# The shift of the norms on ScalarE and VectorE alone, and a weight split moved behind the variance, in a four-layer diffusion backbone on one core

## What is computed

```python
mod_c = (sc @ ada_w[i] + ada_b[i]).reshape(6, D_MODEL)
hc = _rmsnorm(xc, norm_w[i, 0]) * (1.0 + mod_c[1]) + mod_c[0]
...
xc = xc + mod_c[2] * oc
hc = _rmsnorm(xc, norm_w[i, 1]) * (1.0 + mod_c[4]) + mod_c[3]
xc = xc + mod_c[5] * _conv_ffn(hc, ffn_w_up[i], ffn_conv_w[i], ffn_conv_b[i], ffn_w_down[i])
```

## Time and profile before

| what | us |
|---|---|
| median of 3 runs | 1853.62 |
| lowest and highest of them | 1853.53 and 1855.74 |
| the profiled execution | 1852.23 |
| its span | 1850.4 |
| busy: TensorE | 1800.7 |
| busy: VectorE | 1389.0 |
| busy: ScalarE | 986.3 |
| busy: GpSimd | 176.0 |

### The profile page before, as it was taken

The page is one execution under the profiler, slowest core; times in us unless marked ns, Lnnn a source line. Parts: engine busy times, 40 slices in busy tenths (PEclk is TensorE's granted clock), DMA queues, the critical chain, the costliest instruction groups (busy, mean ns, idle before and its releaser), DMA issues.

```text
span 1850.4 us, 27379 instructions
## 1 busy us (share of the span) xinstructions
PE 1800.7 (97%) x11032; PEld 1497.5 (81%) x11032; DVE 1389.0 (75%) x2064; ACT 986.3 (53%) x1492; POOL 176.0 (10%) x147
## 2 busy tenths in 40 slices
PE   5999999999999989999999999999999999999998
PEld 2988877798888867888977678888888787878888
DVE  3865677668898766999855588988765777769984
ACT  2754444545674454766445466744654445547763
POOL 2100121001000113000101110002100220020001
PEclk8999999999999999999999999999999999999999
DMA  8565656867656757675574776566555645545542
GB/s 369 193 229 194 213 206 227 317 231 283 258 217 216 285 207 288 255 290 189 215 299 179 296 290 277 201 224 258 212 197 175 228 180 213 176 165 200 194 175 84
DMA packets 74175, 421.28 MB, mean 228 GB/s; under 512 B 12384, under 2 KB 18936, under 8 KB 26432
## 3 DMA queue, kind: packets, MB, share of 16 engines
q1 hardware_dynamic: 55440, 392.98, 56.8%
q10 hardware_dynamic: 18608, 26.55, 4.3%
HBM read 408.51 MB, written 10.96 MB: 227 GB/s over the span
## 4 chain that ended last, share of the span: by engine, by line
PE 88%; DVE 6%; issue 2%; ACT 2%; DMA 1%; POOL 1%; POOLq 0%; DVEq 0%; ACTq 0%; SPq 0%
PE ps L652 18%; PE ps L674 9%; PE ps L709 9%; PE ps L655 9%; PE ps L634 6%; PE ps L690 5%; PE ps L712 4%; PE ps L637 3%; PE ps L753 3%; PE ps L620 3%; PE ps L622 3%; PE ps L621 3%; DVE spl_lo L498 1%; DMA raw<-in_stream 1%; PE ps L960 1%
## 5 line engine op out<-in xcount | busy, mean ns | idle before, releaser
L498 DVE TENSOR_TENSOR spl_lo<-raw,spl_hi 128x1024 fp32r<-128x1024 f32 x556 | 691.2, 1269 | 150.8 <-ACT spl_hi L487 149.3
L487 ACT ACTIVATE spl_hi<-raw 128x1024 fp32r<-128x1024 f32 x556 | 574.1, 1053 | 286.8 <-PE ps L712 109.5
L652 PE MATMUL ps<-H,spl_hi 128*128 128x512 f32 x1408 | 444.3, 397 | 3.7 <-DVE H L1847 2.4
L655 PEld LDWEIGHTS ps<-H,spl_lo 128*128 128x128 f32 x1408 | 264.5, 188 | 62.5
L655 PE MATMUL ps<-H,spl_lo 128*128 128x256 f32 x1408 | 276.7, 278 | 0.0
L652 PEld LDWEIGHTS ps<-H,spl_hi 128*128 128x128 f32 x1408 | 214.3, 189 | 18.5 <-issue 16.5
L709 PE MATMUL ps<-G,spl_hi 128*128 128x512 f32 x528 | 165.8, 395 | 0.0
L634 PE MATMUL ps<-B,spl_hi 128*128 128x512 f32 x512 | 160.8, 395 | 0.0
L620 PE MATMUL ps<-H,spl_hi 128*128 128x256 f32 x512 | 149.1, 291 | 5.8 <-DVE H L1852 3.3
L621 PE MATMUL ps<-H,spl_hi 128*128 128x256 f32 x512 | 146.0, 285 | 0.0
L622 PE MATMUL ps<-H,spl_lo 128*128 128x256 f32 x512 | 146.0, 285 | 0.0
(11 more groups left out here) (255 smaller groups left out, 2944.3 us busy)
## 6 DMA issues: line engine op xcount, KB each, us to landing
raw<-in_stream SPq DMA_DIRECT2D x366, 1024.0 KB, 5.0
out_new_C<-c_stage ACTq DMA_DIRECT2D x16, 512.0 KB, 3.8
column<-in_ada_cols SPq DMA_DIRECT2D x16, 512.0 KB, 5.3
ada_b<-in_ada_b ACTq DMA_DIRECT2D x4, 768.0 KB, 9.5
cond_all<-cond_out ACTq DMA_DIRECT2D x3, 1024.0 KB, 4.9
E<-rows_out ACTq DMA_DIRECT2D x8, 256.0 KB, 4.3
Em<-rows_out ACTq DMA_DIRECT2D x8, 256.0 KB, 4.6
x<-in_x ACTq DMA_DIRECT2D x1, 1024.0 KB, 11.7
```

Source lines behind the costliest of these rows:

```text
L487: act.activation(spl_hi[m % SPL][:, :], raw[r % RAW][:, h * HALF:(h + 1) * HALF], ACT.Copy).then_inc(S["hi_done"], 1)
L498: dve.tensor_tensor(spl_lo[m % SPL][:, :], raw[r % RAW][:, h * HALF:(h + 1) * HALF], spl_hi[m % SPL][:, :].bitcast(F32), ALU.subtract).the ...
L652: pe.matmul(banks[:, b * 512:(b + 1) * 512], spl_hi[m % SPL][:, c], H[:, kk * 512:(kk + 1) * 512], start=kk == 0, stop=False, skip_group_c ...
L655: mm = pe.matmul(banks[:, b * 512:b * 512 + TOK], spl_lo[m % SPL][:, c], H[:, kk * 512:kk * 512 + TOK], start=False, stop=kk == KD - 1, sk ...
```

## The change

- `norm` of ScalarE: in norms 1 to 7 groups 1 to 3 are made as group 0 was, four activations of a block with the shift as bias (after: L1299), behind VectorE's multiply (`hm_done`). In norm 0 nothing changes.
- `norm` of VectorE: four instructions (hf + shift) - high for groups 1 to 3 of these norms (after: L1862) in place of one subtraction.
- `norm` of GpSimd: the adds of these groups are gone. It keeps the squares and the pow.
- In `project` with nk = KD, in its last step, only half 0 of the next tile's low part is made. Half 1 comes in `inverse_rms`, behind `var` and ahead of the wait for the roots. This concerns the first FFN tile of layers 1 and 2, norms 3 and 5.

```diff
--- before.py
+++ after.py
@@ -1293,8 +1293,14 @@
                                 act.wait_ge(S["hm_first"], 2 * (q - 1) + c // 2 + 1)
                             act.activation(first_block(c, 0), hf[0][:, c * T:(c + 1) * T], ACT.Identity,
                                            bias=coef_b[:, c:c + 1]).then_inc(S["hfirst_hi"], 1)
+                    elif q:
+                        act.wait_ge(S["hm_done"], chunks(q, g))
+                        for c in range(4):
+                            ins = act.activation(first_block(4 * g + c, 0), hf[g % 2][:, c * T:(c + 1) * T], ACT.Identity,
+                                                 bias=coef_b[:, 4 * g + c:4 * g + c + 1])
+                        ins.then_inc(S["hhi_done"], 1)
                     else:
-                        act.wait_ge(S["hf_done"], chunks(q, g))
+                        act.wait_ge(S["hf_done"], g + 1)
                         copy(beside(H, g, 0), v3(hf[g % 2][:, :], TOK), "hhi_done")
                     if late and g == 1:
                         state(1, MH - 1, range(3, 4))
@@ -1828,6 +1834,8 @@
                 link.wait()
                 dve.wait_ge(S["ssq_mm"], q + 1)
                 dve.tensor_scalar(var[:, :], MISC[:, 0:NS], 1.0, D * EPS, ALU.mult, ALU.add).then_inc(S["xvar_done"], 1)
+                if q % 2 and MIXER[q // 2] != "mlstm":
+                    split_lo(dve, INDEX["ffn_up", q // 2, 0], (1,))
                 dve.wait_ge(S["rbc_mm"], q + 1)
 
             def normal(out, src, g):
@@ -1849,6 +1857,13 @@
                             ins.then_inc(S[("h_first", "h_done")[k]], 1)
                         return
                     dve.wait_ge(S["hhi_done"], chunks(q, g))
+                    if q:
+                        for c in range(4):
+                            ins = dve.scalar_tensor_tensor(first_block(4 * g + c, 1), hf[g % 2][:, c * T:(c + 1) * T],
+                                                           coef_b[:, 4 * g + c:4 * g + c + 1],
+                                                           first_block(4 * g + c, 0).bitcast(F32), ALU.add, ALU.subtract)
+                        ins.then_inc(S["h_done"], 1)
+                        return
                     dve.tensor_tensor(beside(H, g, 1), v3(hf[g % 2][:, :], TOK), beside(H, g, 0).bitcast(F32),
                                       ALU.subtract).then_inc(S["h_done"], 1)
 
@@ -1888,7 +1903,7 @@
             def project(n0, count, nk, r, begin=0, columns=None, dots_of=None):
 
                 for t in range(begin, count):
-                    split_lo(dve, n0 + t + 1)
+                    split_lo(dve, n0 + t + 1, (0,) if nk == KD and t + 1 == count else (0, 1))
                     if t == begin and columns is not None:
                         columns()
                     if (dots_of, t) in COLUMN_UNITS:
@@ -2470,8 +2485,8 @@
                 square_total(q)
                 pool.wait_ge(S["xvar_done"], q + 1)
                 pool.tensor_tensor(rstd[:, :], var[:, :], half_pow[:, :], ALU.pow).then_inc(S["rstd_done"], 1)
-                for g in range(1 if q else 0, 4 if shift else 0):
-                    pool.wait_ge(S["hm_done"], chunks(q, g))
+                for g in range(0 if q else 4):
+                    pool.wait_ge(S["hm_done"], g + 1)
                     t = v3(hf[g % 2][:, :], T)
                     pool.tensor_tensor(t, t, coef_b[:, 4 * g:4 * g + 4].unsqueeze(2).to_broadcast([P, 4, T]),
                                        ALU.add).then_inc(S["hf_done"], 1)
```

## The result

| | us |
|---|---|
| before, median of 22 runs | 1853.47 |
| changed kernel, median of 22 runs | 1856.06 |
| ratio, with its 95% interval | 1.0015 (1.0009 to 1.0021) |
| span of the profiled execution, before and after | 1850.4 and 1854.8 |

A forecast was written before the change was run, and what follows sets the result against it. TensorE, 88% of the chain that ended last, was taken as the bound. The shift's -2.5, the late split's +2.4 and the clock's +1.5 gave +1.4 us on the median 1853.62: 1855.0 us, range 1851.8 to 1859.2.

The forecast's parts named there:

- the likeliest case: Whole kernel: gains in the other norms, losses in norms 3 and 5 and a clock loss sum to +1.4 us; chance 0.72.
- part 1: Norms 1, 2, 4, 6, 7: with GpSimd's adds gone the groups of H complete earlier and TensorE waits less, -2.5 us.
- rival 4: Whole change: it does not do what it says; excluded by the order of instructions, no chance of its own.
- Part 2, the load: Norms 3 and 5: SyncE's load waits for the late split, delaying the first FFN matmul by +1.3 and +1.1 us.
- the following weight tiles have some microseconds to spare: Norm 3, behind the late load: next loads queue at about 2.4 us each, yet later weight tiles are not waited for.
- a sign of being wrong: Any norm: TensorE waits on a low half where there is no such wait before; no size given.
- signs of being right: Norms 3 and 5: among others, TensorE idle 2 us and more ahead of the second fill tile, pow of 1.6 us.
- Part 2, the pow: Norm 3: GpSimd's pow waits out the late split, roots start at 733.35 instead of 733.04, hidden behind the late load.
- The term of +1.5: Norms 3 and 5: TensorE's added idle time brings a low clock onto FFN matmuls in one of the two, +1.5 us.
- the late load is not waited for: Norms 3 and 5: the fill tile comes in time and both norms gain, total 1848.1 to 1849.7 us; chance 0.06.
- VectorE becomes the bound: All changed norms: VectorE's extra low-part instructions, 1.3 us more per norm, cancel the gain, total 1857.5 us; chance 0.08.
- "The clock" in both norms: Norms 3 and 5: low clock over the first FFN matmuls, 1.5 us a stretch, total 1858.0 to 1859.5 us; chance 0.14.

The follow-up runs named there:

- The extra subtraction: Changed kernel with both low halves split at the old place and an unread 128x1024 VectorE subtraction behind var in norms 3 and 5; ratio to before 1.0002.
- the shift alone: Changed kernel with both edits of the late half split undone, GpSimd's adds still gone; ratio to before 0.9989, 2.0 us faster.

## Why the prediction held, and where it was off

The direction of the likeliest case (+1.4 us) and the range were right, and the measured +2.8 us, twice as large, lies within the 0.2% that it named. That the total came so near is partly luck: part 1 gained 0.4 us more than forecast, and norms 3 and 5 and two stretches of attention cost more. Point by point:

- **What bounds the kernel**: right. TensorE's busy time did not change in the sum, and the loss of norms 3 and 5 begins with waits of TensorE for the load and the pow.
- **Part 1**: the chain was right to 0.04 us in every group, and GpSimd's busy time fell from 176.0 to 151.9 us, so rival 4 (the edit not doing what it says) is out. The gains: norm 2 -0.8 for -0.5, norm 4 -1.2 for -0.8, norm 6 -0.7 for -0.9, norm 7 -0.1 for -0.2, norm 1 -0.1 for -0.1. The sum of -2.9 for -2.5 is well met. In norms 2 and 4 I had let the following weight split take back more than it did: ScalarE too was free 0.9 us earlier, and the split moved along.
- **Part 2, the load**: right in mechanism. First FFN matmul of norm 3: shift +1.2 us, for +1.3. **The step that was too short is "the following weight tiles have some microseconds to spare".** They had none in norm 3. The load of the second FFN tile queued behind the late ones, beside a load of `ada_b` from ScalarE's queue; its low half was waited for, 0.63 us. Norm 3 cost +2.1 in place of +1.3. A wait on a low half where there was none is what the prediction itself had listed as a sign of being wrong. One of its signs of being right failed as well: it wanted 2 us and more of idle TensorE ahead of the second fill tile in both norms, and norm 3 has 1.08, since the late roots (1.02) and the low clock on the first fill tile (1.94 for 1.06) had used up the rest; norm 5 has 2.72.
- **Part 2, the pow**: 1.61 us for 0.70, and the roots held up. The sentence "the 0.3 us of the roots are hidden" was right for this kernel. The extra subtraction shows the wait without the late load, at 2.4 us in all, the clock's share in it not separated.
- **The clock**: one low stretch fell on the second fill tile and the first FFN matmuls of norm 5, 0.50 in 1080 to 1082: the tile took 1.94 us in place of 1.06, and norm 5 cost +2.3 in place of +1.1. The term of +1.5 met about +1.2 there, but not as it was meant. Before had one low stretch in each of these norms and so has the changed kernel: none came on top in these norms, and the one of norm 5 moved onto the late tile. And "most of this is beside waits" was wrong of before: in the trace of the shift alone the stretches are missing, and norms 3 and 5 are 1.3 and 1.9 us shorter, most of it on the roots and the fill tiles. That another would come in the attention of layer 1, +0.7, was not foreseen, for I looked for the clock only where the change was.
- **Rivals**: "the late load is not waited for" fell with 1.08 and 2.72 us of wait. "VectorE becomes the bound" fell with the shift alone at 0.9989. "The clock" in both norms did not come: the stretch in norm 3 fell on the first fill tile, which took 1.94 us, in front of a wait.

The Trainium skill, "SBUF — State Buffer", section Who interferes with whom, gives the exclusive lock between a GpSimd instruction that reads SBUF and a VectorE instruction with two SBUF inputs; both traces agree, with 1.61 us against 0.70 for a pow of 128x2, and four blocks in 1.13 us against 1.92 once the adds are gone.

## What to carry to other kernels

In such a ring a buffer is given back by the last step that reads it. Who moves that step behind a wait moves every load that is queued on the buffer; so find the tile that comes into it, and who takes it first, before filling an idle engine. A small GpSimd operation on the critical path can pay for most of a VectorE instruction with two SBUF inputs that starts just ahead of it: 1.61 us for 0.70 here. Where an engine's order holds DMA issues between two groups of a norm, try them on a queue that is idle: by the trace 0.92 us of issue cost 0.9 us of TensorE here, though the times do not separate the two kernels. And where an effect is a few microseconds, see whether the profiled execution is a typical one before its trace is added up.

## What was not expected of the hardware

- A GpSimd pow on 128x2 elements took 1.61 us behind a VectorE subtraction of 128x1024 and 0.70 us without it. The trace of before had no such pair, so the size was new; it came out alike with two different VectorE instructions.
- The granted clock was 0.50 at the same places, within 0.4 us, in three profiles of one kernel (near 733.7 and 1071.6), and at others in variants whose timing differed by less than 2 us there. From one profile it looked like a matter of luck. It is not luck alone, but the mean clocks of the other executions show that it is not fixed either.
- Loads of 1 MB issued with no other under way landed in 4.65 to 5.0 us in norms 3 and 5. In norm 3 of the changed kernel the late one took 4.7 us and the four behind it 6.8, 10.1, 10.6 and 11.9. In the attention of layer 2 two took 7.8 and 7.7 where before took 6.5 and 6.3, unexplained.
